# First stage of a transformer kernel taken in parts, late parameter loads moved to the next stage, and the result turned and stored in quarters between the last products

## The chip, the cores and the metric

One Trainium2 chip, of which the program uses one core. The metric is the time of one execution in device microseconds (us). Three runs of the kernel before took 1059.59, 1060.05 and 1061.69 us; the median is 1060.05 us.

The engines are called by these names: PE is TensorE (matrix products and transposes), PEld its weight loads, DVE is VectorE, ACT is ScalarE, POOL is GpSimd, SP is SyncE, which here only issues DMA transfers. A name with q (SPq, PEq) is an engine's sequencer.

## What is computed

Six blocks run one after the other on x of 256 tokens by 1024 features, all in float32: a forget-gated attention block (fox), a sparse attention block (NSA), then a gated recurrence (HGRN2), a feed-forward block, a latent attention block (MLA) and a second feed-forward block. Each adds to x. Only the two ends matter here:

```python
def rmsnorm(x, g):
    xf = x.astype(jnp.float32)
    y = xf * lax.rsqrt(jnp.mean(xf * xf, axis=-1, keepdims=True) + NORM_EPS)
    return (y * g.astype(jnp.float32)).astype(x.dtype)

def fox_mixer(h, w_in, b_f, w_out):
    proj = h @ w_in
    q, k, v, f, z = jnp.split(proj, [W, 2 * W, 3 * W, 3 * W + N_HEADS], axis=-1)
    ...
    log_f = jax.nn.log_sigmoid(f.astype(jnp.float32) + b_f.astype(jnp.float32))
    c = jnp.cumsum(log_f, axis=1).transpose(0, 2, 1)
    ...
```

The program begins with `h = rmsnorm(x, norm_g[0])` and `h @ w_in`, and ends with `x + hidden @ w_down` of the last feed-forward block, which is the output.

## The kernel before

**Layout.** x is kept turned: 128 features on the partitions, 8 chunks of features by 256 tokens. A weight tile is 1 MB, 128 x 2048 float32, that is 8 chunks of 128 rows by 256 columns. A product in float32 is made of three (`product3`, L444): both factors are split into a high part, rounded to the fast type float32r, and a low part, the remainder, and high*high, high*low and low*high are added up. So each weight tile passes through a ring of three slots: SP loads it (`load`, L356), ACT copies it to the high part (`high`, L388), DVE subtracts to get the low part (`low`, L404; `low_half`, L412, half a tile), and PE multiplies: 48 products of 128 x 256 for a tile (`by_feature`, `by_token`). SP loads the tile three places on when the low part has been taken.

**Norms.** `Norm` (L566) does not wait for the root of the mean square: it splits x times gain (`high` L577, `low` L583), multiplies, and scales the product by the row of inverse roots afterwards. For the sum, ACT squares x in four pieces (`square`, L593), POOL adds them (`add_squares`, L605), PE adds over the partitions with a column of ones (`sums`, L620), ACT takes the root (`root`, L631), DVE the inverse and a half of it (`finish`, L643), and PE spreads it over a row (`spread`, L670), which DVE copies (L664).

**Stages.** The program is a row of blocks with a function for each engine. At the end of a block all engines wait for each other. Inside a block the order of each engine is written out by hand, with semaphores between them.

**The first block (L1277 to L1350).** SP loads constants, x with tokens on the partitions, and tiles 0 to 2, then the weights of the forget gate `w_f`, its bias `b_f`, late constants and tiles 3 and 4. ACT's queue issues the load of `norm_g` and then 13 small loads of late parameters. PE runs 12 products of zeros (`keep_warm`, L553), turns the `norm_g` parameters (L1271), turns x (16 transposes, L1327), runs 12 more products of zeros, multiplies tile 0 and sums the squares. DVE copies the turned x from PSUM to SBUF (L1342), takes the low parts of h (L586), of tiles 0 and 1 (L409), and multiplies `w_f` by the gain (L1349). ACT takes the high parts of h (L580) and of tile 0 (L399), squares x (L594), takes the high part of tile 1 and loads the table of the root (L603).

**The second block (fox, from L1402)** multiplies tiles 1 to 15 (n is the tile). A function `between` or `quarter` is called after each half or quarter of a tile's products, and puts other work of PE there: the spread of the root, the product with `w_f` in three parts (`forget_product`, L1431), the running sums of the log gates (`c_sums`, L1417), the turning of their three bf16 parts (`c_turn`, L1424), and the steps of attention, from tile 3 on. The first of these waits for `c_ready`, a row that DVE copies (L1582). DVE's order there is: the gate's steps (L1555 to L1562), low part of tile 3, the split of the sums (`split_c`, L1566 to L1576), low part of tile 4, evacuation of tile 2 (L1529, L1530), the row c (L1582). POOL clears `c_parts` and `kz` (L1411, L1412) at the start of the block, and SP first loads the convolution parameters (L1262).

**The end.** In the last feed-forward block `last_down` (L1054) multiplies the last tile, two chunks of the output at a time, into banks 4 to 7; DVE adds each pair to x (L1233). Then the block ends, and a last block turns x back (16 transposes, L2910), copies four banks (L2918) and stores the result in two transfers of 512 KB (L2925).

## Time and profile before

| | us |
|---|---|
| median of three runs | 1060.05 |
| the three runs | 1059.59 to 1061.69 |
| the profiled execution, its own time | 1060.7 |
| its span, first to last instruction | 1058.9 |
| PE busy | 1021.7 (96%) |
| DVE busy | 766.7 (72%) |
| ACT busy | 549.6 (52%) |
| POOL busy | 69.7 (7%) |
| mean granted TensorE clock | 0.997 of full |

How to read it: a busy share is an average over all stages, and a matmul record runs until its modelled end, so overlapping records make PE look busy without a gap. Starts are counted from the start of the span. "Idle before" in brackets is the time in which the engine stood still before the row, and what ended it. The profiled execution took 0.65 us more than the median of the runs; 1.8 us of its time lie outside the span.

### The profile page before, as it was taken

Reading aid. Unit: us, or ns where it says so; the run is one execution under the profiler, and the core shown is the slowest. Engines: PE = TensorE matmul, PEld = TensorE weight load, DVE = VectorE, ACT = ScalarE, POOL = GpSimd, SP = SyncE. Lnnn points to the kernel's source line nnn. Section 1 sums busy time; section 2 is a strip of 40 time slices with the busy share of each in tenths; the row PEclk is TensorE's granted clock in tenths of the full one; section 3 lists DMA queues with packets and bytes.
Section 4 is the critical chain, followed back from the end, with each engine's and each line's share of the span. In section 5 each row is a group of like instructions: output and inputs, shape, how many; then the busy total and the mean of one; then the engine's idle time right before and its main releaser. Section 6 shows DMA issues by size and latency. Waiting matters only on the chain. (4 is left out here: it accounts for less than half of the span.)

```text
span 1058.9 us, 20362 instructions
## 1 busy us (share of the span) xinstructions
PE 1021.7 (96%) x8176; PEld 964.8 (91%) x8178; DVE 766.7 (72%) x1300; ACT 549.6 (52%) x869; POOL 69.7 (7%) x54
## 2 busy tenths in 40 slices
PE   7999999999899999999999999999998899999997
PEld 5988899997677999999999999999997899999997
DVE  5656676867677667498667878787866559887785
ACT  5544455455555556553555545454674555545441
POOL 4000005000000220000020000000001320000000
PEclk9999999999999999999999999999999999999999
DMA  8544345892111456600464766565531347565641
GB/s 278 160 132 144 123 127 168 225 291 82 40 41 54 146 173 187 199 1 1 138 182 121 206 190 182 175 198 160 146 119 40 93 127 210 170 200 172 198 144 40
DMA packets 184141, 153.08 MB, mean 145 GB/s; under 512 B 12477, under 2 KB 176900, under 8 KB 184068
## 3 DMA queue, kind: packets, MB, share of 16 engines
q1 hardware_dynamic: 183858, 152.01, 47.8%
q8 instruction: 51, 0.84, 0.3%
q14 instruction: 22, 0.18, 0.1%
q10 hardware_dynamic: 210, 0.05, 0.0%
HBM read 148.91 MB, written 1.05 MB: 142 GB/s over the span
## 5 line engine op out<-in xcount | busy, mean ns | idle before, releaser
L447 PE MATMUL bank<-h_high,w_high 128*128 128x256 f32 x1312 | 378.8, 289 | 6.3 <-DVE ffn_normed L1090 2.6
L448 PE MATMUL bank<-h_low,w_high 128*128 128x256 f32 x1312 | 370.9, 283 | 0.0
L449 PE MATMUL bank<-h_high,w_low 128*128 128x256 f32 x1312 | 370.9, 283 | 0.0
L399 ACT ACTIVATE w_high<-ring 128x2048 fp32r<-128x2048 f32 x137 | 261.5, 1911 | 165.4 <-PE bank L449 161.5
L409 DVE TENSOR_TENSOR w_low<-ring,w_high 128x2048 fp32r<-128x2048 f32 x118 | 271.2, 2299 | 32.8 <-ACT w_high L399 32.4
L447 PEld LDWEIGHTS bank<-h_high,w_high 128*128 128x128 f32 x1312 | 251.1, 191 | 13.5 <-issue 9.9
L448 PEld LDWEIGHTS bank<-h_low,w_high 128*128 128x128 f32 x1312 | 251.3, 192 | 0.7 <-issue 0.5
L449 PEld LDWEIGHTS bank<-h_high,w_low 128*128 128x128 f32 x1312 | 251.2, 191 | 0.0
L447 PE MATMUL bank<-ffn_hidden_high,w_high 128*128 (+1 forms) x352 | 99.8, 283 | 2.0 <-DVE ffn_hidden_low L1123 2.0
L448 PE MATMUL bank<-ffn_hidden_low,w_high 128*128 (+1 forms) x352 | 99.6, 283 | 0.0
L449 PE MATMUL bank<-ffn_hidden_high,w_low 128*128 (+1 forms) x352 | 99.6, 283 | 0.0
L1077 ACT ACTIVATE ffn_conv<-ffn_normed,par 128x256 f32<-128x256 f32 x88 | 48.0, 593 | 68.6 <-DVE ffn_normed L1090 68.4
L1099 DVE SCALAR_TENSOR_TENSOR ffn_conv<-ffn_normed,par,ffn_conv 128x254 f32<-128x254 f32 (+1 forms) x176 | 77.1, 480 | 7.4 <-ACT ffn_conv L1077 2.3
L792 ACT ACTIVATE work<-bank,work 128x128 f32<-128x128 f32 (+1 forms) x112 | 47.6, 430 | 61.6 <-DVE work L774 48.5
L611 POOL TENSOR_TENSOR h<-h 128x512 f32<-128x512 f32 x15 | 38.4, 2557 | 484.2 <-ACT h L594 483.9
L447 PEld LDWEIGHTS bank<-ffn_hidden_high,w_high 128*128 128x128 f32 x352 | 67.6, 192 | 2.3 <-issue 2.3
L449 PEld LDWEIGHTS bank<-ffn_hidden_high,w_low 128*128 128x128 f32 x352 | 67.6, 192 | 0.0
L448 PEld LDWEIGHTS bank<-ffn_hidden_low,w_high 128*128 128x128 f32 x352 | 67.6, 192 | 0.0
L774 DVE TENSOR_REDUCE work<-bank 128x2 f32<-128x256 f32 (+2 forms) x64 | 32.4, 507 | 38.1 <-PE bank L759 37.8
L754 PE MATMUL bank<-work 128*128 128x256 f32 (+2 forms) x160 | 54.2, 438 | 1.9 <-ACT work L792 1.9
L418 DVE TENSOR_TENSOR w_low<-ring,w_high 128x1024 fp32r<-128x1024 f32 x40 | 48.6, 1221 | 7.1 <-ACT w_high L399 7.0
L447 PE MATMUL bank<-w_high,h_high 128*128 128x256 f32 x160 | 46.6, 291 | 2.9 <-DVE w_low L409 2.9
(352 smaller groups left out, 1750.4 us busy)
## 6 DMA issues: line engine op xcount, KB each, us to landing
ring<-in_ffn_w_up_dram SPq DMA_DIRECT2D x44, 1024.0 KB, 6.0
ring<-in_ffn_w_down_dram SPq DMA_DIRECT2D x22, 1024.0 KB, 5.0
ring<-in_fox_w_in_dram SPq DMA_DIRECT2D x16, 1024.0 KB, 5.7
ring<-in_hgrn_w_in_dram SPq DMA_DIRECT2D x16, 1024.0 KB, 5.4
ring<-in_nsa_w_in_dram SPq DMA_DIRECT2D x14, 1024.0 KB, 5.5
ring<-in_fox_w_out_dram SPq DMA_DIRECT2D x4, 1024.0 KB, 5.0
ring<-in_nsa_w_out_dram SPq DMA_DIRECT2D x4, 1024.0 KB, 5.0
ring<-in_hgrn_w_out_dram SPq DMA_DIRECT2D x4, 1024.0 KB, 5.0
```

Source lines behind the costliest of these rows:

```text
L399: i = nc.scalar.activation(dst, src, ACT.Copy)
L409: ops.tensor_tensor(w_lo[:, t % NSLOT, :], ring[:, t % NSLOT, :], w_hi[:, t % NSLOT, :].bitcast(F32), ALU.subtract).then_inc(low_in[t % NS ...
L418: i = nc.vector.tensor_tensor(w_lo[:, t % NSLOT, q], ring[:, t % NSLOT, q], w_hi[:, t % NSLOT, q].bitcast(F32), ALU.subtract)
L447: nc.tensor.matmul(o, ah, bh, start=start, stop=False, **kw)
L448: nc.tensor.matmul(o, ah, bl, start=False, stop=False, **kw)
L449: return nc.tensor.matmul(o, al, bh, start=False, stop=stop, **kw)
L611: ops.tensor_tensor(h[:, 0:2, :], h[:, 0:2, :], h[:, 2 * i:2 * i + 2, :], ALU.add).then_inc(n_added, 1)
L754: nc.tensor.matmul(o, q, k, start=(i == 0), stop=False)
L774: i = nc.vector.tensor_reduce(least, self.bank(u), AX.X, ALU.min)
L792: i = nc.scalar.activation(pb[:, e, 0:unit["w"]], ps[:, e, :], ACT.Exp, scale=unit["scale"][1] if unit.get("scale") else -1.0, bias=self.l ...
L1077: i = nc.scalar.activation(y[:, j % 2, e, :], un[:, j % 2, e, :], ACT.Identity, scale=column(cw + 4 * FC, e, j, later), bias=column(cb, e, ...
L1099: i = nc.vector.scalar_tensor_tensor(out=dst, in0=un[:, j % 2, e, 0:S - back], scalar=column(cw + (2 - back) * 2 * FC, e, j, later), in1=d ...
```

## The change

- The first block is taken in parts. x and tiles 0 and 1 are loaded in halves, each with a semaphore. `keep_warm` runs 9, 2 and 10 products of zeros in place of 12 and 12. ACT and DVE read the turned x straight from PSUM for the high and low parts of h; the copy to SBUF comes later (`place`). Tile 0 is split in quarters, and its products wait for a quarter each.
- The norm of the first block: ACT squares x in the layout of tokens, in two instructions that also add up along the row, and takes the root. POOL's additions, PE's sums and the root in the second block are gone. The inverse is taken in the first block (`invert`), the row in the second (`take_row`). The table of the root is loaded first.
- The 13 late parameter loads move from ACT's queue in the first block to SP's queue in the second, after the load of tile 4, which moves into the second block as well. The product of `w_f` and the gain moves to DVE's second block.
- In the second block the spread comes before tile 1, the three parts of `forget_product` a quarter of a tile later, `c_sums` after three quarters of tile 2 (before: half), and `c_turn` after the first quarter of tile 3 (before: at the end of tile 2).
- The last block is gone. `turn_result` turns a pair of chunks back between the products of `last_down`, ACT copies it (`place_result`), and SP stores it: four transfers of 256 KB, in rows of 1 KB.

```diff
         def keep_warm(n):
...
-                nc.tensor.matmul(B[5][:, :], zeros_bf[:, 0:P], zeros_bf[:, :], start=True, stop=True)
+                nc.tensor.matmul(B[2][:, :], zeros_bf[:, 0:P], zeros_bf[:, :], start=True, stop=True)
...
                     elif o % 2:
                         mm.then_inc(down_done, 1)
+                    if not following and o % 2 and o > 1:
+                        turn_result(pe, o // 2 - 1)
+
+            def turn_result(pe, i):
+
+                pe.wait_ge(x_added, 4 * l + i + 1)
+                for tt in range(TT):
+                    for c in range(2):
+                        mm = nc.tensor.transpose(B[i][:, (2 * tt + c) * P:(2 * tt + c + 1) * P],
+                                                 x[:, 2 * i + c, tt * P:(tt + 1) * P], ident)
+                mm.then_inc(res_turned, 1)
+
+            def place_result(act, i):
+                act.wait_ge(res_turned, i + 1)
+                nc.scalar.activation(res[:, :, i * 256:(i + 1) * 256], B[i][:, :].rearrange("p (t d) -> p t d", t=TT),
+                                     ACT.Copy).then_inc(res_in, 1)
+
+            def store_result(sp, i):
+                sp.wait_ge(res_in, i + 1)
+                sp.dma_start(out[0].rearrange("(t p) d -> p t d", p=P)[:, :, i * 256:(i + 1) * 256],
+                             res[:, :, i * 256:(i + 1) * 256]).then_inc(stored, 16)
...
+        def fox_first(pe):
+
+            def ready(c):
+                nrm_fox.chunk(pe)(c)
+                if c == 6:
+                    in_parts(pe, f0)
+                elif c % 2 == 0:
+                    pe.wait_ge(part_low, c // 2 + 1)
...
             @block.scalar
             def _(act):
                 load_params(act, (0,), loaded_p)
-                act.wait_ge(cleared, 1)
-                n_late.append(load_params(act, (1,), loaded_p2))
-                for i in range(4):
-                    nrm_fox.high(act, i)
-                high(act, 0)
-                for i in range(4):
-                    nrm_fox.square(act, i)
-                high(act, 1)
+                act.wait_ge(cleared, 2)
                 nrm_fox.table(act)
+                act.wait_ge(p_placed, 1)
+                for c in range(DC):
+                    if c % 2 == 0:
+                        act.wait_ge(turned, c // 2 + 2)
+                    nc.scalar.activation(h_hi[:, c, :], xt(c), ACT.Copy, scale=nrm_fox.gain[:, c:c + 1])\
+                        .then_inc(n_high, 1)
+                for q in range(4):
+                    if q == 0:
+                        act.wait_ge(half_in[0], 16)
+                    if q == 2:
+                        landed(act, 0)
+                    nc.scalar.activation(quarter(w_hi, q), quarter(ring, q), ACT.Copy)\
+                        .then_inc(high_in[0] if q == 3 else part_high, 1)
+
+                def square_tokens(tt):
+                    nc.scalar.activation(h[:, 4 * tt:4 * tt + 4, :].rearrange("p c t -> p (c t)"), x_tok[:, tt, :],
+                                         ACT.Square, accum_out=rstd[:, tt:tt + 1]).then_inc(squared, 1)
...
             @block.tensor
             def _(pe):
                 pe.wait_ge(cleared, 2)
-                keep_warm(12)
+                keep_warm(9)
...
-                pe.wait_ge(x_placed, 4)
-                keep_warm(12)
+                    if c == 3:
+                        keep_warm(2)
+                keep_warm(10)
                 fox_first(pe)
-                nrm_fox.sums(pe)
 
             @block.vector
             def _(dve):
...
+                for c in range(DC):
+                    if c % 2 == 0:
+                        dve.wait_ge(n_high, c + 2)
+                    nc.vector.scalar_tensor_tensor(out=h_lo[:, c, :], in0=xt(c), scalar=nrm_fox.gain[:, c:c + 1],
+                                                   in1=h_hi[:, c, :].bitcast(F32), op0=ALU.mult,
+                                                   op1=ALU.subtract).then_inc(n_split, 1)
+                for q in range(4):
+                    dve.wait_ge(high_in[0], 1) if q == 3 else dve.wait_ge(part_high, q + 1)
+                    nc.vector.tensor_tensor(quarter(w_lo, q), quarter(ring, q), quarter(w_hi, q).bitcast(F32),
+                                            ALU.subtract).then_inc(low_in[0] if q == 3 else part_low, 1)
...
+                place(0)
+                place(1)
+                dve.wait_ge(part_high, 4)
+                low_half(dve, 1, 0, ready=True)
+                place(2)
+                low_half(dve, 1, 1)
+                place(3)
+                nrm_fox.invert(dve)
...
             @block.sync
             def _(sp):
-                n_late.append(load_params(sp, range(2, 6), loaded_p2))
+                load(sp, NSLOT + 1)
+                n_late.append(load_params(sp, range(1, 6), loaded_p2))
...
                 pe.wait_ge(narrowed, 1)
+                nrm_fox.spread(pe)
...
-                    if (n, half) == (2, 0):
-                        c_sums()
-                    if (n, half) == (2, 1):
-                        c_turn()
...
                 def quarter(n, q):
-                    if (n, q) == (1, 0):
-                        nrm_fox.spread(pe)
-                    if n == 1 and q < 3:
-                        forget_product(q)
+                    if n == 1 and q:
+                        forget_product(q - 1)
+                    if (n, q) == (2, 2):
+                        c_sums()
+                    if (n, q) == (3, 0):
+                        c_turn()
...
-                nrm_fox.finish(dve)
+                nrm_fox.take_row(dve)
+                dve.wait_ge(fl, 32)
+                nc.vector.tensor_tensor(w_f[:, :, :], w_f[:, :, :], bcast(pc("norm_g", 0, DC), 2, FOX_H),
+                                        ALU.mult).then_inc(w_f_ready, 1)
```

How the instructions stand. VectorE's first block before:

```order
L1339 COPY par<-bank 128x16 [waits params_turned]
L1342 COPY x<-bank 128x512 [waits x_turned] x4
L586 SCALAR_TENSOR_TENSOR h_low<-x,par,h_high 128x256 [waits norm_high_ready] x8
L409 TENSOR_TENSOR w_low<-ring,w_high 128x2048 [waits w_high_ready0]
L409 TENSOR_TENSOR w_low<-ring,w_high 128x2048 [waits w_high_ready1]
L1349 TENSOR_TENSOR w_f<-w_f,par 128x128 [waits fox_f_loaded]
L1277 UNCONDITIONAL_BRANCH
```

And in the change, from the last low part of h on (`bank` is the turned x in PSUM):

```order
L1442 SCALAR_TENSOR_TENSOR h_low<-bank,par,h_high 128x256
L1447 TENSOR_TENSOR w_low<-ring,w_high 128x512 [waits first_weights_high] x3
L1447 TENSOR_TENSOR w_low<-ring,w_high 128x512 [waits w_high_ready0]
L1451 COPY x<-bank 128x512 x2
L419 TENSOR_TENSOR w_low<-ring,w_high 128x1024 [waits first_weights_high]
L1451 COPY x<-bank 128x512
L419 TENSOR_TENSOR w_low<-ring,w_high 128x1024 [waits w_high_ready1]
L1451 COPY x<-bank 128x512
L666 RECIPROCAL rstd<-rstd 128x2 [waits norm_root]
L668 TENSOR_SCALAR rstd_half<-rstd 128x2 [waits norm_inverse]
L1351 UNCONDITIONAL_BRANCH
```

The four copies of x stood ahead of everything and now stand behind tile 0, up to the end of the block, and the inverse root stands behind them.

TensorE at the turning of the parts of c, tile 2 to tile 3, before:

```order
L449 MATMUL bank<-h_high,w_low 128x256
L1427 MATMUL bank<-ident_bf,work 128x128 [waits c_split_step]
L1427 MATMUL bank<-ident_bf,work 128x128
L447 MATMUL bank<-w_high,h_high 128x256 [waits bank_free1,w_low_ready0]
L448 MATMUL bank<-w_low,h_high 128x256
```

and in the change (the three rows ahead of L1538 are the last of the first twelve products of tile 3):

```order
L448 MATMUL bank<-w_high,h_high 128x256
L449 MATMUL bank<-w_low,h_high 128x256
L450 MATMUL bank<-w_high,h_low 128x256
L1538 MATMUL bank<-ident_bf,work 128x128 [waits c_split_step]
L1538 MATMUL bank<-ident_bf,work 128x128
L448 MATMUL bank<-w_high,h_high 128x256
```

The two small products moved from ahead of tile 3 to behind its twelfth product; the first attention step stands behind the twenty-fourth in both.

TensorE's end, before:

```order
L448 MATMUL bank<-ffn_hidden_low,w_high 128x256
L449 MATMUL bank<-ffn_hidden_high,w_low 128x256
L1137 UNCONDITIONAL_BRANCH
L2905 UNCONDITIONAL_BRANCH [waits barrier_Pool_Activation_PE_DVE_SP_release]
L2910 MATMUL bank<-cst,x 128x128 x16
```

and in the change:

```order
L450 MATMUL bank<-ffn_hidden_high,w_low 128x256
L1087 MATMUL bank<-cst,x 128x128 [waits ffn_added_to_x]
L1087 MATMUL bank<-cst,x 128x128 x3
L1087 MATMUL bank<-cst,x 128x128 [waits ffn_added_to_x]
L1087 MATMUL bank<-cst,x 128x128 x3
L1168 UNCONDITIONAL_BRANCH
```

Eight of the sixteen transposes stand behind the last product, and eight more, in two groups of four, now stand between the products ahead of it.

## Rows read from the trace of the kernel before

**Rows 1.** The page, busy time and share of the span by engine.

```profile
PE 1021.7 (96%) x8176; PEld 964.8 (91%) x8178; DVE 766.7 (72%) x1300; ACT 549.6 (52%) x869; POOL 69.7 (7%) x54
```

**Rows 2.** Timeline of the first 16 us: start, duration, engine, line, count, idle before.

```profile
1.50 4.16 PE L557 MATMUL bank<-zeros_bf 128*128 128x512 bf16 x12 [1.50 <-POOL eps L1295]
...
6.69 1.97 PE L1327 MATMUL bank<-cst,work 128*128 128x128 f32 x16 [0.87 <-DMA work<-in_x_dram]
...
8.11 3.30 ACT L580 ACTIVATE h_high<-x,par 128x256 fp32r<-128x256 f32 x8 [0.69 <-DVE x L1342]
...
9.78 3.25 DVE L586 SCALAR_TENSOR_TENSOR h_low<-x,par,h_high 128x256 fp32r<-128x256 f32 x8
...
13.12 2.17 ACT L594 ACTIVATE h<-x 128x512 f32<-128x512 f32 x4
...
13.24 2.29 DVE L409 TENSOR_TENSOR w_low<-ring,w_high 128x2048 fp32r<-128x2048 f32 x1 [0.21 <-ACT w_high L399]
...
15.59 0.39 PE L447 MATMUL bank<-w_high,h_high 128*128 128x256 f32 x1 [2.90 <-DVE w_low L409]
```

**Rows 3.** The same view from the last product of stage one, 21 to 25 us.

```profile
21.48 1.05 PE L627 MATMUL bank<-cst,h 128*128 128x1 f32 x8
...
23.00 0.36 PE L447 MATMUL bank<-h_high,w_high 128*128 128x256 f32 x1 [0.47 <-PEq L1277]
...
23.06 3.52 POOL L1412 MEMSET work<- 128x4096 f32 x1
...
23.48 3.13 DVE L660 TENSOR_SCALAR rstd_half<-rstd 128x2 f32<-128x2 f32 x1
...
24.50 0.60 PE L562 MATMUL bank<-cst,rstd 128*128 128x128 f32 x4
```

**Rows 4.** The same view, second to fourth tile of the fox stage, 30 to 43 us.

```profile
30.27 1.19 PE L1435 MATMUL bank<-w_f,x 128*128 128x16 f32 x10
...
32.83 0.28 PE L447 MATMUL bank<-h_high,w_high 128*128 128x256 f32 x1
...
34.27 2.29 DVE L409 TENSOR_TENSOR w_low<-ring,w_high 128x2048 fp32r<-128x2048 f32 x1
...
35.71 0.29 PE L1419 MATMUL bank<-work,cst 128*128 128x16 f32 x2
...
37.59 2.29 DVE L409 TENSOR_TENSOR w_low<-ring,w_high 128x2048 fp32r<-128x2048 f32 x1
...
39.35 0.36 PE L447 MATMUL bank<-w_high,h_high 128*128 128x256 f32 x1
...
41.22 0.42 DVE L1582 CAST work<-bank 128x256 bf16<-128x256 f32 x1
...
42.31 0.59 PE L754 MATMUL bank<-work 128*128 128x256 f32 x2
```

**Rows 5.** The same view, from the last product of the program to its end.

```profile
1051.56 0.69 DVE L1233 TENSOR_TENSOR x<-bank,x 128x512 f32<-128x512 f32 x1 [0.74 <-PE bank L449]
...
1052.57 1.94 PE L2910 MATMUL bank<-cst,x 128*128 128x128 f32 x16 [1.05 <-PEq L1137]
...
1053.23 2.48 DVE L2918 COPY work<-bank 128x512 f32<-128x512 f32 x4 [0.98 <-PE bank L2910]
...
1054.55 1.55 SPq L2925 DMA_DIRECT2D out_dram<-work  x2
```

**Rows 6.** Busy time in a stretch: length, engines, granted clock, DMA share, GB/s.

```profile
1057.50:1058.00 0.50, 0.00 (x0) 0.00 (x0) 0.00 (x0) 0.00 (x0) 0.00 (x0) 1.00 0.99 401
```

**Rows 7.** Timeline around 201.6 us, VectorE and GpSimd.

```profile
201.60 2.29 DVE L409 TENSOR_TENSOR w_low<-ring,w_high 128x2048 fp32r<-128x2048 f32 x1
...
201.74 0.53 POOL L1732 MEMSET work<- 128x512 f32 x1 [20.66 <-DVE blocks_low L2032]
```

**Rows 8.** Timeline of SyncE's queue: single issues of small loads.

```profile
9.70 2.98 SPq L1286 DMA_DIRECT2D b_f<-in_fox_b_f_dram  x1
...
22.81 0.73 SPq L1262 DMA_DIRECT2D prow<-in_ffn_conv_w_dram  x2
```

More of the change, by code:

```diff
@@ L410, in low, with low_half @@
                               ALU.subtract).then_inc(low_in[t % NSLOT], 1)
-        def low_half(dve, t, half):
+        def low_half(dve, t, half, ready=False):
             if t >= NT:
                 return
-            dve.wait_ge(high_in[t % NSLOT], t // NSLOT + 1)
+            if not ready:
+                dve.wait_ge(high_in[t % NSLOT], t // NSLOT + 1)
             q = slice(half * SLOT // 2, (half + 1) * SLOT // 2)
@@ L1146, in _ @@
                         load(sp, t)
+                    if not following:
+                        for i in range(4):
+                            store_result(sp, i)
+                        sp.wait_ge(stored, 64)
                 @block.tensor
@@ L1194, in _ @@
                     next_high(act, t0 + NTILE)
+                    if not following:
+                        for i in range(4):
+                            place_result(act, i)
                     if following:
@@ L1274, in build, with load_halves, quarter, xt @@
         f0, fz = T["fox"], T["fox_z"]
-        fox_first = tile_first(f0, by_token)(nrm_fox)
+        plan_tile(f0)
+        def fox_first(pe):
[5 more added lines that the diff above has]
+                    pe.wait_ge(part_low, c // 2 + 1)
+            w = parts(f0, "p (c n) -> p c n", c=DC, n=256)
+            for tt in range(TT):
+                for c in range(DC):
+                    if tt == 0:
+                        ready(c)
+                    mm = product3(pbank(f0)[:, tt * 256:(tt + 1) * 256],
+                                  [v[:, c, tt * P:(tt + 1) * P] for v in hsp], [v[:, c, :] for v in w],
+                                  c == 0, c == DC - 1)
+            mm.then_inc(tile_done, 1)
+        def load_halves(sp, t):
+            for half in range(2):
+                k = slice(4 * half, 4 * half + 4)
+                sp.dma_start(slot(t, DC, 256)[:, k, :], tiles[t][0][:, k, :])\
+                    .then_inc(w_loaded[t % NSLOT] if half else half_in[t], 16)
+        def quarter(r, q):
+            return r[:, 0, q * SLOT // 4:(q + 1) * SLOT // 4]
+        def xt(c):
+            return B[4 + c // 2][:, (c % 2) * S:(c % 2 + 1) * S]
         fl, w_f_ready = sem("fox_f_loaded"), sem("fox_f_weights_ready")
@@ L1287, in _ @@
                 sp.dma_start(cst[:, nfirst:], cst_dram[:, nfirst:ncst]).then_inc(loaded_c2, 16)
-                for t in range(NSLOT, NSLOT + 2):
-                    load(sp, t)
+                load(sp, NSLOT)
             @block.gpsimd
@@ L1340, in _ @@
[L1340 to L1350 removed]
+                dve.wait_ge(turned, 1)
```

115 lines of the change are left out of this document (53 added, 62 removed).

## The prediction

> **What bounds the kernel now.** I read the page first: PE is busy 96% of the span, DVE 72%, ACT 52% [rows 1]. So between the ends of the program only PE's own stream counts, and a change there gains where PE stands still or runs something that is no product. Then I read the timeline of the first 16 us [rows 2]. The reader is to see a chain in which PE multiplies nothing until 15.59: x has landed at 6.6 (PE's idle time before its transposes ends on that load), DVE copies it, ACT takes eight high parts, DVE eight low parts, ACT the high part of tile 0, DVE its low part, one whole step after the other. Next the seam of stages one and two [rows 3]: sums of squares, 1.05 us, then 0.47 us for the barrier, and tile 1 begins at 23.00. Then tiles 2 and 3 [rows 4], where the order of small work moves, and the end [rows 5]: after the last add PE waits for the barrier, turns x, DVE copies, and SP stores 1 MB, with the span ending at 1058.9. Everything between these places keeps its instructions. I take it to last as long as before; what is gained or lost at the ends goes through in full.
>
> **Stage one, up to the first product.** The 12 products of zeros take 4.16 us, the last at short spacing [rows 2]; nine end near 5.0, and the parameters are turned by 5.2. The first half of x lies between then and 6.6, when all of x had landed; I take 5.4, since it is the first half of the bytes behind the same constants. Sixteen transposes take 1.97 us, so the first pair of chunks is turned at 6.1; ACT's eight high parts at 0.41 us (3.30 for eight) then run without a gap to 9.4. The quarters of the high part of tile 0 are 128 x 512 like the four squares that took 2.17 us, so 0.54 each: 9.95, 10.5, 11.0, 11.6. DVE's low parts (3.25 for eight) follow ACT's and end at 10.3. A quarter of the low part lies between 0.57 (a quarter of 2.29 [rows 2]) and 0.69 (128 x 512 alone [rows 5]); I take 0.63. The first quarter is ready at 10.95 and the first product starts at 11.05, where it was 15.59: **4.5 us earlier**. The other quarters come every 0.63 us and PE uses one in 0.72 (six products at 0.12), so it doesn't wait again. The halves of tile 0 were not waited for before, when ACT began the tile at 11.3; that they are there at 9.4 and 10.5 is likely but unseen (rival 3).
>
> **Stage one, its end.** PE finishes 48 products, 5.76 us, at 16.8. ACT, free at 11.6, has two squares of 128 x 1024 (1.3 each with the read of the sum, an estimate from 0.54 for half the size), two halves of tile 1 (1.0 each) and a root: 16.4. DVE is later. From the last quarter, 12.8, it has four copies of x (2.48, as the four of the same form [rows 5]), two halves of a low part (2.4), the inverse and its half (0.35): 18.05. So DVE, not PE, opens the barrier, and PE stands still for 1.25 us. With the 0.47 us of the seam [rows 3] PE spreads the root at 18.5 and starts tile 1 at 19.05. Before, tile 1 began at 23.00 and lost another 0.45 to the spread inside it [rows 3]. **Gain 4.4 us**; the sums, 1.05 us, are in it. Bounds: 5.6 if DVE's tail were no longer than PE's, 2.9 if the first product came 1.5 later.
>
> **Stage two.** Three waits are at stake. First, `w_f`: its product with the gain now stands behind DVE's copy of the row, beside POOL's long memset. A DVE operation of two columns was held by that memset from 23.48 to its end, 3.13 us [rows 3]. But a subtraction of two SBUF operands ran its usual 2.29 us across another memset [rows 7], and `w_f` is of that form; so it is ready at 20.0, and PE asks at 19.05 + 2.88 = 21.9. I put 0; held, it would be ready at 22.4 and cost 0.5. Second, the removed additions of POOL and root of ACT are off the path. Third, the sums of c, **which I take as a loss**. Before, tile 1 to tile 2 took 9.83 us; now 9.35, so tile 2 starts at 28.4. The gate's product used to end at 31.46, 1.4 before tile 2 [rows 4]; now its third part ends with tile 1, at 28.55. The low part of tile 3 began 2.81 later and takes 2.29 [rows 4]: 33.65. `c_sums` starts after 36 products, at 32.7, and is done at 33.45, so the split (1.1) runs to 34.8. From the start of the low part of tile 4 to the end of the row c it was 37.59 to 41.64 [rows 4], 4.05 us: now 38.85. PE starts tile 3 at 34.8 and is at the first attention step 2.96 + 0.1 later, 37.9. Before, the row had 0.67 us to spare; now PE waits **1.0 us** (bounds: 0 if the low part of tile 3 hides better, 1.6 if the gate's steps on ACT come late). After it DVE has slack again.
>
> **The late loads.** The 13 small loads left ACT's queue before ACT had work: nothing gained. On SP they go ahead of tile 5, whose load waited until 28.9 for DVE's low part of tile 2 anyway, and now may start at 22.7. Two such issues took 0.73 us [rows 8]; 19 take 7 us from 18.8, to 25.8. Tile 5 is multiplied near 50. **0**. If this cover were gone see rival 5.
>
> **The end.** Two groups of four transposes lie between products: 0.45 each (1.94 for sixteen [rows 5]), so the last product ends 0.9 later, at 1052.4. The third group runs under DVE's last add. The add ends at 1053.15, the last group is turned at 1053.85 (1052.57 to 1053.23 for four before), ACT copies in 0.6, and SP issues at 1054.55, when it used to issue the first of two stores of 512 KB; the second went out 1.2 later [rows 5]. Data flowed at 401 GB/s up to 1058.0 [rows 6], 0.9 before the end; 1.05 MB at that rate is 2.6 us, so it began at 1055.4, 0.85 after the issue. The last quarter then flows from 1055.4 for 0.65, and the end is at 1056.95. **Gain 1.9 us**, bounds 0.6 (rate of a third) and 2.5.
>
> The Trainium skill speaks against quarters: "DMA: Bandwidth & Descriptors", section "Bandwidth", wants transfers of 1 MiB and measured 138 GB/s at 64 KB against 341 at 1 MB. By the lower figure the last quarter would flow 1.9 us (an estimate), and the gain at the end would be 0.65; no row here shows a store of this size.
>
> **Sum.** 4.4 - 1.0 + 1.9 = 5.3 us. Against the profiled execution, 1060.7, that is 1055.4; this one was 0.65 above the median of the runs, 1060.05, so the predicted median is **1054.8**.
>
> **Rivals.**
> 1. *The forecast*, 1054.8: chance 0.62.
> 2. *PE itself ends stage one.* DVE's copies and halves overlap more than I add up, and the row c isn't waited for: 5.6 + 1.9 = 7.5, so 1052.5. For it: 0.67 us to spare before. Against: DVE's list is in order, with durations from its own rows. Chance 0.10.
> 3. *The parts don't do what they say.* The first product waits for the landing of tile 0, not for its split: loads of one queue share the engines, and a half may land little before the whole. If it is there only at 11.3, the first product starts at 12.5; 1.5 is lost, and the wait for c at its bound takes 0.6 more: gain 3.2, so 1056.9. For it: all we know is that ACT found the tile there at 11.3. Chance 0.14.
> 4. *The quarters store slowly.* At a third of the rate of [rows 6] the last one flows 1.95 us, and the gain at the end is 0.6: total 4.0, so 1056.0. The page named above makes this the expected way. Chance 0.10.
> 5. *Slower: SP's queue holds the weights.* One small load, the bias, held SP for 2.98 us behind weight tiles [rows 8]. If each of the 19 did that behind tile 4, tile 5 would be issued at 18.8 + 57 = 76, not 25.8. PE can bear an issue up to about 39 (product at 50, less 6 for landing and 5 for the split); each us beyond costs one. From 44.5 the whole gain is gone, and at 76 the time is 1060 + 31 = 1092. Against: the six of stage two took under 0.4 each, the bias stood behind three tiles in flight, and now only one is. Chance 0.04.
>
> **Range and chances.** About 0.2% of the time, 2.1 us, is what a measurement here tells from no change: faster is below 1057.9. The range goes from rival 2 with a little more at the end, 1052.3, to rival 3 with the slow quarters, 1057.8. Outside it lie rival 5 and corners of the others. Faster takes rivals 1 to 4 but for their tails: 0.87. The same: tails of 3 and 4 with a wait of 0.5 for `w_f`: 0.09. Slower: rival 5: 0.04.
>
> **What would show it.** The first product of tile 0 near 11.0; DVE's last copy of x near 17.7 and PE idle for some 1.7 us before the spread; tile 1 near 19.0; the first attention step with an idle time of about 1 us that ends on the row c; the last store issued near 1051.2 (1054.55 less 3.4), and a span near 1053.6. I am wrong if DVE isn't what opens the barrier, if the wait at c is missing or over 2 us, if the last store needs over 3 us, or if PE is short of weights after tile 4.

## The result, and the profile after

| | before | changed |
|---|---|---|
| median, us (six executions each) | 1060.77 | 1054.2 |
| lowest to highest | 1059.59 to 1061.69 | 1052.91 to 1057.88 |
| profiled execution: its own time | 1060.7 | 1052.91 |
| its span | 1058.9 | 1051.1 |
| its mean granted clock of TensorE | 0.997 | 1.000 |

The ratio is 0.9944, with a 95% interval of 0.9925 to 0.9962: **faster by 5.9 us (4 to 8)**; the medians are 6.6 apart. Forecast was 1054.8, 5.3 less than before.

The busy line of the page, against [rows 1]: POOL loses the additions of the first norm (7.0 us), DVE has 6.8 us less and ACT 1.5 more.

```profile
PE 1017.8 (97%) x8167; PEld 960.9 (91%) x8167; DVE 759.9 (72%) x1300; ACT 551.1 (52%) x875; POOL 62.7 (6%) x51
```

The timeline of the first stage, rows of PE, ACT and DVE (start, length, engine, line, operation, idle time before and what ended it), against [rows 2, 3]:

```profile
6.06 1.09 PE L1426 MATMUL bank<-cst,work 128*128 128x128 f32 x8 [0.73 <-DMA work<-in_x_dram]
6.81 3.08 ACT L1389 ACTIVATE h_high<-bank,par 128x256 fp32r<-128x256 f32 x8 [4.12 <-PE bank L1426]
7.77 3.23 DVE L1442 SCALAR_TENSOR_TENSOR h_low<-bank,par,h_high 128x256 fp32r<-128x256 f32 x8 [2.24 <-ACT h_high L1389]
9.76 2.20 ACT L1396 ACTIVATE w_high<-ring 128x512 fp32r<-128x512 f32 x4
10.91 2.49 DVE L1447 TENSOR_TENSOR w_low<-ring,w_high 128x512 fp32r<-128x512 f32 x4
11.74 0.35 PE L448 MATMUL bank<-w_high,h_high 128*128 128x256 f32 x1 [0.86 <-DVE w_low L1447]
...
17.38 0.68 DVE L1451 COPY x<-bank 128x512 f32<-128x512 f32 x1
...
18.17 0.17 DVE L668 TENSOR_SCALAR rstd_half<-rstd 128x2 f32<-128x2 f32 x1
18.79 0.68 PE L563 MATMUL bank<-cst,rstd 128*128 128x128 f32 x4 [1.07 <-PEq L1351]
18.85 3.53 POOL L1523 MEMSET work<- 128x4096 f32 x1
19.97 0.29 DVE L1660 TENSOR_TENSOR w_f<-w_f,par 128x128 f32<-128x128 f32 x1
```

The chain of before, one whole step after the other, is now overlapped: ACT has begun the weights at 9.76, before DVE has ended the low parts of h. The first product is at 11.74 (15.59 before), and DVE is the last to reach the barrier, at 18.34. The product for `w_f` takes 0.29 us in the middle of POOL's memset.

Tiles 2 and 3, DVE and PE, against [rows 4]:

```profile
31.50 2.28 DVE L409 TENSOR_TENSOR w_low<-ring,w_high 128x2048 fp32r<-128x2048 f32 x1
...
32.94 0.29 PE L1530 MATMUL bank<-work,cst 128*128 128x16 f32 x2
...
34.61 0.18 DVE L1688 CAST work<-work 128x32 bf16<-128x32 f32 x1
34.83 2.29 DVE L409 TENSOR_TENSOR w_low<-ring,w_high 128x2048 fp32r<-128x2048 f32 x1
37.03 0.68 DVE L1638 TENSOR_TENSOR work<-bank,rstd_row 64x512 f32<-64x512 f32 x1
...
38.45 0.42 DVE L1694 CAST work<-bank 128x256 bf16<-128x256 f32 x1
38.93 0.70 PE L762 MATMUL bank<-work 128*128 128x256 f32 x2 [0.67 <-DVE work L1694]
```

A wait that before had not: PE stands 0.67 us at the first attention step until DVE has copied the row c. The end, against [rows 5]:

```profile
1046.53 0.69 DVE L1273 TENSOR_TENSOR x<-bank,x 128x512 f32<-128x512 f32 x1 [1.18 <-PE bank L450]
1047.27 0.66 PE L1087 MATMUL bank<-cst,x 128*128 128x128 f32 x4 [0.35 <-DVE x L1273]
1047.97 0.60 ACT L1093 ACTIVATE h<-bank 128x512 f32<-128x512 f32 x1 [0.41 <-PE bank L1087]
1048.59 0.37 SPq L1098 DMA_DIRECT2D out_dram<-h  x1
```

From the start of the last add to the end of the span it is 4.6 us, where it was 7.3.

**Where the 7.8 us between the two spans lie.** I took DVE's and ACT's instructions that both traces have, in order, and their difference in start: 3.26 us earlier from tile 3 on, 3.32 at 520, 3.59 from 527 on, then 5.88 from 839 on, and 7.8 at the end. Nothing was changed between 45 and 1040. The 0.27 us at 527 are one start of ACT (L2310 before, L2422 now), 0.37 us behind DVE's result before and 0.09 now. The late start stands in all four profiles with the old first stage and in none of the ten with the new one, so that it is gone comes with the new start; why, no run here tells. The 2.3 us between 800 and 839 are the granted clock of TensorE. Windows of before, with PE's busy time and the clock (1.00 is 2.4 GHz, 0.50 is 1.2 GHz), around the places where it fell (length, PE, clock, share of the DMA engines, GB/s):

```profile
803.00:806.00 3.00, 1.20 (x7) 1.00 0.00 0
806.50:809.90 3.40, 3.38 (x14) 0.50 0.00 0
828.00:830.00 2.00, 1.26 (x9) 1.00 0.00 0
830.40:833.80 3.40, 3.39 (x16) 0.50 0.62 184
```

In the profile of the changed kernel the clock doesn't fall. So on an even clock the change is worth 7.8 - 2.3 = 5.5 us: 3.3 at the start, 0.3 at 527, 1.9 at the end. And its six spans rise as the mean clock falls: 1051.1 at 1.000, 1051.3 and 1052.0 at 0.999, 1052.9 at 0.998, 1054.4 at 0.996, 1056.1 at 0.994.

### The profile page after: what moved, and what is told of

It is laid out like the page before. It is cut to its first block and busy times, and to the rows that moved or that the text cites. A ratio compares the mean times of both kernels' runs of the same rounds, so it can differ in the third digit from the quotient of the medians.

```text
span 1051.1 us, 20343 instructions
## 1 busy us (share of the span) xinstructions
PE 1017.8 (97%) x8167; PEld 960.9 (91%) x8167; DVE 759.9 (72%) x1300; ACT 551.1 (52%) x875; POOL 62.7 (6%) x51
## 5 line engine op out<-in xcount | busy, mean ns | idle before, releaser
L399 ACT ACTIVATE w_high<-ring 128x2048 fp32r<-128x2048 f32 x135 | 257.7, 1912 | 164.9 <-PE bank L450 157.8
L409 DVE TENSOR_TENSOR w_low<-ring,w_high 128x2048 fp32r<-128x2048 f32 x116 | 265.9, 2294 | 32.1 <-ACT w_high L399 31.8
L613 POOL TENSOR_TENSOR h<-h 128x512 f32<-128x512 f32 x12 | 31.6, 2631 | 473.7 <-ACT h L596 473.7
L419 DVE TENSOR_TENSOR w_low<-ring,w_high 128x1024 fp32r<-128x1024 f32 x42 | 51.0, 1219 | 7.1 <-ACT w_high L399 7.0
```

The lines of the kernel that those rows point to most:

```text
L399: i = nc.scalar.activation(dst, src, ACT.Copy)
L409: ops.tensor_tensor(w_lo[:, t % NSLOT, :], ring[:, t % NSLOT, :], w_hi[:, t % NSLOT, :].bitcast(F32), ALU.subtract).then_inc(low_in[t % NS ...
L419: i = nc.vector.tensor_tensor(w_lo[:, t % NSLOT, q], ring[:, t % NSLOT, q], w_hi[:, t % NSLOT, q].bitcast(F32), ALU.subtract)
L613: ops.tensor_tensor(h[:, 0:2, :], h[:, 0:2, :], h[:, 2 * i:2 * i + 2, :], ALU.add).then_inc(n_added, 1)
```

## Experiments

My theory was the prediction's own: start 3.4, end 1.9, the two independent. One rival was that the two parts hang together or that something else had given the time; another, from the comparison of the traces, that the clock was part of the change. All "even clock" figures are spans without stretches at half clock: a profile's span, less what the shift of its instructions against another profile shows for such a stretch or for a late x. For before that is 1058.9 - 2.3 = 1056.6. All runs from e6 on, and e4, start from the changed kernel.

**e1: before once more**, unchanged.

> The kernel before, once more, for the granted clock of each execution. In the profile of before, the clock stood at half for two stretches of 3.4 us near 806 and 830, in the profile of the changed kernel nowhere; the shift of DVE's and ACT's instructions between the two traces goes from 3.6 to 5.9 us across them. Theory A (those 2.3 us are chance, and the change is worth 5.5 on an even clock): the spans of before scatter from about 1056.6 (no such stretch) up, in steps that go with the mean clock, as those of the changed kernel scatter from 1051.1 at clock 1.000 to 1056.1 at 0.994; time by clock is one line for both kernels, 5.5 us apart. Theory B (the change itself removes the stretches): before never shows a clock above 0.998, and the two stretches stand at the same places in this profile.

Median 1060.06, ratio 0.9998. In this profile the clock is at half from 379.6 to 383.0, in a stage where before's first profile had none, and DVE's instructions behind it are 2.4 us later. So place and number differ from execution to execution: theory B's fixed places are wrong. Yet B was right on a point: no execution at 0.999 or above. That called for e5.

**e2: the new start with the old end. e3: the old start with the new end.** The diff of each is the other half of the change:

```diff
 # e2: as before
+                for tt in range(TT):
+                    sp.wait_ge(res_in, 2 * tt + 2)
+                    sp.dma_start(out[0, tt * P:(tt + 1) * P, :], res[:, tt, :]).then_inc(stored, 16)
 # e3: as in the change
+                        for i in range(4):
+                            store_result(sp, i)
```

> The new first stage, new order of tiles 1 to 3 and moved loads, with the end of before. My theory (start 3.3 to 3.6, end 1.9, nothing else): on an even clock the span is 1051.1 + 1.9 = 1053.0; first product 11.7, attention step 38.9 as in the profile of the changed kernel. A rival, that the two parts are not independent (the late loads or the changed places of tiles shift the ring and cost or gain something far behind): span on an even clock off 1053.0 by over 0.5.

> The old first stage, with the result turned and stored in quarters between the last products. My theory: on an even clock 1056.6 - 1.9 = 1054.7, with every instruction up to the last tile where it was before, and from the last add to the end of the span 4.6 us (1046.53 to 1051.1 in the changed kernel) where before took 7.3 (1051.56 to 1058.9). Rival, that the quarters pay only beside the new start: less than 1.5.

e2: median 1056.86, ratio 0.9960 (0.9947 to 0.9973). The profile ran at clock 1.000 with span 1054.5; the second half of x landed late, which made the start 1.42 us later, so 1053.0: as forecast. That rests on this correction; the lowest of its spans was 1053.9. e3: median 1058.18, ratio 0.9981 (0.9972 to 0.9990); its 11 spans lie between 1056.2 and 1058.4, none with a mean clock above 0.998. In its profile the clock fell in the first tile (windows as above):

```profile
14.00:17.30 3.30, 1.32 (x11) 1.00 1.01 266
17.30:20.70 3.40, 3.40 (x19) 0.50 0.90 289
```

From 23 to 806, where the clock of before falls, everything is 1.74 us later than in before: 0.39 of it because x landed late, 1.35 by that stretch. So on an even clock and with x as in before it is 1054.7: as forecast. The two halves add up: 3.9 and 2.6 us by the medians, 6.5 together.

**e4: row c ahead of the low part of tile 4.**

```diff
                 split_c()
-                low(dve, nc.vector, f0 + 4)
                 evacuate(2)
                 dve.wait_ge(c_turned, 1)
                 nc.vector.tensor_copy(c_row, B[7][:, 0:S]).then_inc(c_ready, 1)
+                low(dve, nc.vector, f0 + 4)
```

> The changed kernel, but DVE takes the evacuation of tile 2 and the row c before the low part of tile 4, not behind it. If what PE waits for at the first attention step (0.67 us, ended by the row) is only DVE's order: the row is ready at about 37.3 (turned parts at 36.9 + 0.42), PE starts the step at 38.26 without a wait and everything behind it is 0.67 earlier, as long as the low part of tile 4 (now done near 39.6) is there before PE asks for it near 41. Span on an even clock 1050.4. Rival: the low part of tile 4 or the reductions of attention are late instead, and the gain is given back within the next two tiles: 1051.1 or more.

PE and DVE of this profile, where everything up to here is 0.20 us earlier than in the changed kernel:

```profile
36.61 0.42 DVE L1693 CAST work<-bank 128x256 bf16<-128x256 f32 x1
37.06 2.29 DVE L409 TENSOR_TENSOR w_low<-ring,w_high 128x2048 fp32r<-128x2048 f32 x1
...
37.90 0.59 PE L762 MATMUL bank<-work 128*128 128x256 f32 x2
```

The step has no idle time before it, and from here on everything is 1.15 us earlier than in the changed kernel, 0.95 beyond the 0.20: the wait is DVE's order, and it is gone, with nothing late behind it in the stage. It is more than the 0.67 in the bracket, which counts from the modelled end of the product before. Without a wait the step starts 0.83 sooner, at 37.90, and its first products are 0.11 shorter. The median, 1054.74, shows none of it: the profile has three stretches at half clock (374, 804, 828), and three of the six executions stand below 0.998.

**e5: before, with more zeros ahead of the first product.**

```diff
                 pe.wait_ge(x_placed, 4)
-                keep_warm(12)
+                keep_warm(24)
```

> The kernel before, with 24 instead of 12 products of zeros behind the turned x, so that PE isn't idle for 2.9 us before the first product. So far no execution of a kernel with the old first stage (45 with its clock) had a mean clock above 0.998, and the profile with the new end alone had the clock at half from 17.3 to 20.7, after PE had been busy 1.32 of 3.3 us; of 17 with the new first stage 5 stood at 0.999 or 1.000. Theory A: that idle time is why the clock falls in the first tile, and the new first stage gains by removing it, beside its 3.3 us: here no stretch at half near 17, several executions at 0.999 or 1.000, the lowest span near 1056.6 and the median 1 to 1.4 us below that of before. Theory B, the fall near 17 has another cause or is chance: nothing above 0.998, median unchanged. The first product stays at 15.6 in both.

```profile
14.00:17.30 3.30, 2.99 (x19) 1.00 1.07 268
17.30:20.70 3.40, 3.40 (x31) 1.00 0.91 291
```

Four of 11 executions ran at 1.000, with spans of 1056.7 to 1057.1, the even clock that was worked out for before (1056.6). Of the 17 executions of before that ran beside them one did (1056.5), and of all 77 with the old first stage that same one. So the full clock was kept more often with the zeros. That they do it by preventing a fall at 17 is not shown. The same windows of the first profile of before, with PE idle from 12.69 to 15.59, have the full clock too, and so has e1:

```profile
14.00:17.30 3.30, 1.71 (x14) 1.00 1.12 280
17.30:20.70 3.40, 3.40 (x30) 1.00 0.86 284
```

There the clock fell at 806 and 830, in e1 at 380, and at 17 in e3 alone. The median of e5 is only 0.5 below that of before, and the ratio 1.0000 (0.9990 to 1.0009): the gain that I expected of it, 1 to 1.4, isn't shown. Where the clock fell in its other executions, no profile tells.

**e6: two copies of x on ACT.**

```diff
                 low_half(dve, 1, 0, ready=True)
-                place(2)
                 low_half(dve, 1, 1)
-                place(3)
 # ACT, behind its root
+                act.wait_ge(n_split, DC)
+                for i in (2, 3):
+                    nc.scalar.activation(x[:, 2 * i:2 * i + 2, :], B[4 + i][:, :]..., ACT.Copy)
```

> The changed kernel, but the last two copies of x out of PSUM are made by ACT, behind its root, not by DVE. My theory is that DVE (its last instruction ends at 18.34, PE's last product at 17.7) opens the barrier: DVE then ends near 17.2, ACT near 17.5, PE's 17.7 decides, the spread moves from 18.79 to 18.15 and tile 1 from 19.23 to 18.6; everything behind is 0.65 earlier, span on an even clock 1050.45 (for x landing when it did in the profile of the changed kernel). Rival, that it is PE's own end and the barrier takes 1.07 us: no change at 18.79.

```profile
16.23 1.07 ACT L1416 ACTIVATE x<-bank 128x512 f32<-128x512 f32 x2
...
16.91 0.17 DVE L668 TENSOR_SCALAR rstd_half<-rstd 128x2 f32<-128x2 f32 x1
...
18.12 0.57 PE L563 MATMUL bank<-cst,rstd 128*128 128x128 f32 x3 [0.47 <-PEq L1351]
```

DVE ends at 17.08, the spread stands 0.47 us behind PE's last product instead of 1.07, and all that follows is 0.67 earlier, of which 0.07 is an earlier first product: 0.60 gained. DVE did open the barrier. The median, 1055.15, is again above that of the changed kernel, with no execution above 0.998.

**e7: x in quarters**, 256 columns each, with a semaphore of its own for each.

> The changed kernel with x loaded in four parts of 256 columns, two chunks each. In the changed kernel the first half landed at 6.01 and the second 1.57 later, and PE waited 0.73 us for the first; ACT began its high parts at 6.81. If the first product hangs on the landing of x, the first quarter is there near 5.25, ACT begins at 6.1, DVE's low parts end 0.7 earlier and the first product is at 11.05 in place of 11.74; tile 1 at 18.55. Rival: shorter rows (1 KB per token) and two more issues make the load slower, the last quarter lands after 8.3 and ACT waits between its pairs: no gain or a loss.

The quarters landed at 4.32, 6.19, 6.96 and 7.65, and:

```profile
6.17 3.20 ACT L1389 ACTIVATE h_high<-bank,par 128x256 fp32r<-128x256 f32 x8 [3.48 <-PE bank L1425]
9.24 1.17 ACT L1396 ACTIVATE w_high<-ring 128x512 fp32r<-128x512 f32 x2
10.70 1.15 ACT L1396 ACTIVATE w_high<-ring 128x512 fp32r<-128x512 f32 x2 [0.29 <-DMA ring<-in_fox_w_in_dram]
...
11.10 0.36 PE L448 MATMUL bank<-w_high,h_high 128*128 128x256 f32 x1 [0.59 <-DVE w_low L1446]
```

First product 11.10, all 0.63 earlier; median 1052.67, ratio 0.9935 (0.9920 to 0.9949). Most of the 0.63 need not be the quarters': in the profile of the changed kernel the first half had landed late, at 6.01. In e9, with halves, it landed at 5.57, and ACT began its high parts at 6.38, against 6.81 there and 6.17 here. That leaves 0.2 to the quarters, and e10 doesn't show even that.

**e8: the store in one go**, two transfers of 512 KB once all four quarters are in.

```diff
-                            store_result(sp, i)
-                        sp.wait_ge(stored, 64)
+                            sp.wait_ge(res_in, i + 1)
+                        for tt in range(TT):
+                            sp.dma_start(out[0, tt * P:(tt + 1) * P, :], res[:, tt, :]).then_inc(stored, 16)
```

> The changed kernel with its transposes and copies between the last products, but the result stored in two transfers of 512 KB once all four quarters are in. If the quarters gain because only 256 KB is left to flow (0.78 us at the 336 GB/s seen for a quarter) and not by the moved transposes: 1.05 MB at the 401 GB/s of before flow 2.6 us, so the end comes 1.8 us later, span on an even clock 1052.9, and nearly all of the 1.9 us of the end are gone. If the transposes and copies were what counted: 1051.5 or less.

Span 1054.6 with one stretch at half clock, behind which everything is 1.57 later than in the changed kernel: even clock 1053.1; the one execution at 1.000 has 1053.3. Median 1055.05, ratio 0.9950 (0.9937 to 0.9964). The gain of the end, 1.9, is gone whole, so it lies in what is left to flow when the last result is there. One window of this store (its length, ACT's busy time, the clock, the DMA engines' share, GB/s) and one of the changed kernel's last quarter (with the busy times of all five engines):

```profile
1052.50:1053.00 0.50, 0.00 (x0) 0.50 1.02 418
```

```profile
1049.50:1050.00 0.50, 0.00 (x0) 0.00 (x0) 0.00 (x0) 0.00 (x0) 0.00 (x0) 1.00 0.99 336
```

**e9: tiles 0 and 1 loaded whole**, `load(sp, t)` for `load_halves(sp, t)`.

> The changed kernel with tiles 0 and 1 loaded whole (one transfer of 1 MB each), as before, and ACT and DVE still working in quarters. In the changed kernel the first half of tile 0 landed at 9.09, the second at 10.60, and ACT began its first quarter at 9.76, when its high parts of h were done. My forecast took the halves for needed; rival 3 of the prediction said that they do nothing. If a whole tile lands when its second half did: ACT begins at 10.6, the first product is at 12.55 instead of 11.74, tile 1 at 20.0, span on an even clock 1051.9. If one transfer lands sooner than two halves (9.6 as in the kernel before, where x was one transfer too): ACT isn't held, and nothing changes.

```profile
10.22 2.19 ACT L1391 ACTIVATE w_high<-ring 128x512 fp32r<-128x512 f32 x4 [0.74 <-DMA ring<-in_fox_w_in_dram]
10.88 2.50 DVE L1441 TENSOR_TENSOR w_low<-ring,w_high 128x512 fp32r<-128x512 f32 x4 [0.32 <-ACT w_high L1391]
...
11.72 0.36 PE L448 MATMUL bank<-w_high,h_high 128*128 128x256 f32 x1 [1.25 <-DVE w_low L1441]
```

The tile landed at 10.2, ACT waited 0.74 us for it and DVE 0.32 more for ACT, and yet the first product is at 11.72 as before: here h was ready 0.44 us sooner, and with halves that would have shown. So my price, 0.8, was too high; the halves are worth the 0.3 of DVE's wait here, 0.4 at most, and DVE's own work hides the rest. The span of the profile is 1051.2, as in the changed kernel; the median of the four executions is 1055.74, ratio 0.9954 (0.9939 to 0.9969), with three of them at 0.997 or 0.998.

**e10: e4, e6 and e7 together. e11: the same, with zeros in the idle places of MLA's attention.**

```diff
+                    if k in (2, 3):
+                        zeros5((2, 5)[k - 2])
...
+                    if k in (4, 16, 18):
+                        zeros5({4: 3, 16: 4, 18: 3}[k])
```

> The changed kernel with the three edits that gained: row c ahead of the low part of tile 4 (0.94 measured at the attention step), two copies of x on ACT (0.66), x in quarters (0.63). If they add up: first product 11.1, PE's last product of tile 0 at 17.05, spread at 17.5, tile 1 at 17.95, the attention step without a wait at 36.75, and the span on an even clock 1051.1 - 2.2 = 1048.9; median by chance of the clock 1.5 to 2 above it. If they stand in each other's way (ACT's two copies end after PE's last product, since ACT has 1.2 us more to do and PE ends earlier): one of the terms is halved, 1049.3.

> The kernel of the run before this one, with 17 products of zeros (0.21 us each) in the five places of the attention of MLA where PE idles: before logits 2 and 3, and before the weighing in steps 4, 16 and 18 (idle 0.54, 1.34, 0.78, 1.25 and 0.98 in the profile of the changed kernel), into a bank that nothing uses there. Three of seven profiles so far have the clock at half near 804 to 810 and 828 to 834. If PE's idle time in front is what lets the clock fall there: no such stretch in this profile, the even-clock span unchanged (1048.9), and fewer executions below clock 0.999, so a median 0.5 to 1 us lower than without the zeros. If not: the same scatter of spans and a median equal within its scatter, or higher by what the zeros delay.

e10: median 1053.12, ratio 0.9926 (0.9912 to 0.9939), profile at 1.000 with span 1049.6, not 1048.9. Behind tile 3 all is 1.63 earlier than in the changed kernel: row c and the copies gave their 0.95 and 0.60, and 0.08 came at the first product; x in quarters gave nothing: the first landed at 4.39, but PE was at its zeros until 5.45. e11: median 1051.83, ratio 0.9920 (0.9907 to 0.9934); by the shift against e10 the zeros delay nothing. That they steady the clock isn't shown: neither profile has a stretch at half before the last store, and the highest span of five is 1051.6 in both.

**e12: fewer zeros at the start**, against e11.

```diff
-                keep_warm(9)
+                keep_warm(6)
...
-                    if c == 3:
+                    if c in (1, 3):
                         keep_warm(2)
```

> The kernel of e11 with 6 instead of 9 products of zeros ahead of the turned parameters, and 2 more behind the first pair of chunks. In e7, e10 and e11 the first quarter of x landed at 4.32 to 4.41, but PE was still at its zeros (until 5.25, 5.45, 5.46; the later, the later the clock first stood at full: 4.99, 6.34, 6.93), so the first high part of ACT came at 6.2 to 6.9. If the zeros now bound the start: the parameters are turned at 4.1, the first pair at 4.5 to 5.2, the last pair follows the landing of the last quarter (7.65), ACT's high parts end near 9.0 instead of 9.9 and the first product is at 10.9 instead of 11.8; PE's last product of tile 0 at 16.7 and tile 1 at 17.75 where it was 18.7; span on an even clock 1048.6 or less. Rival: ACT (free at 17.4 with its two copies) becomes what opens the barrier, so tile 1 only gains 0.4. A second rival: with less work on PE the clock comes to full later and the first tile pays.

```profile
4.18 0.28 PE L1313 MATMUL bank<-cst,prow 16*128 16x16 f32 x1
4.39 0.88 PE L1429 MATMUL bank<-cst,work 128*128 128x128 f32 x4
...
17.21 0.68 PE L563 MATMUL bank<-cst,rstd 128*128 128x128 f32 x4 [0.53 <-PEq L1351]
```

The first product is at 10.69, the spread 1.07 us earlier than in e11. **This version has the lowest median: 1051.15 us of four executions, ratio 0.9904 (0.9886 to 0.9922)**; the interval overlaps that of e11. Its lowest span is 1049.2; by the shift of DVE's instructions against e11, 0.80 of the 1.07 us is left at 192. The stretch at half clock of its profile (373.5) hides the rest of the way; the lowest spans, 1049.2 and 1049.5, don't show the 0.8. The rival, that ACT now opens the barrier, is worth 0.06 us at most: the spread stands 0.53 behind PE's last product, where it was 0.47 in e6.

## Why the prediction was right, point by point

- **First product.** Forecast 11.05, measured 11.74; 4.5 us earlier was 3.85. The term that was mis-sized is the landing of x: I took 5.4 for the first half, it was 6.01 (PE's idle time of 0.73 ends on it). In other profiles it was 5.24 to 5.65, and there the zeros of PE bound the start instead.
- **End of stage one.** DVE ends it, as the prediction said: at 18.34 (18.05), tile 1 at 19.23 (19.05). PE stood idle for 1.07 in front of the spread, where the forecast had 1.25 and 0.47 of barrier, 1.7: PE's last product ended at 17.72, not 16.8, so DVE was only 0.6 behind it. DVE's list from the last quarter on was 0.3 shorter than I added up, which took back half of what the first product was late. Tile 2 began at 28.54, 4.29 earlier; forecast was 4.4. e6 shows the mechanism by taking it away: 0.60. Rival 2, that PE itself ends stage one, is out.
- **`w_f` beside the memset.** Costed at nothing, bound 0.5. Its 0.29 us lie inside the memset of 3.53, and PE doesn't wait for it.
- **The row c.** Forecast was a loss of 1.0, all of it a wait. `c_sums` 32.94 (32.7), end of the split 34.79 (34.8), row ready 38.87 (38.85). The idle time was 0.67, below the 1.0, since PE asked at 38.26, 0.36 later than forecast; the loss as a whole was 4.29 - 3.38 = 0.91, and e4 gave back 0.95.
- **The late loads.** Costed at nothing: 19 issues of 0.25 to 0.55 us from 19.02 to 26.5, and tile 5 issued at 26.56, where it was 28.96 before. Rival 5 is out. (Its price was added up wrongly: 37 us late, less the 5.3 gained, is 1091.7.)
- **The end.** Forecast 1.9 of gain, measured 1.9. From the last issue to the end 2.5 us (forecast 2.4), the quarter flowing at 336 GB/s in its fullest half microsecond. The Trainium skill ("DMA: Bandwidth & Descriptors", section "Bandwidth") gives 138 GB/s at 64 KB and 341 at 1 MB, measured on loads issued from GpSimd, and nothing between. This kernel's stores of 256 KB, issued from SP, are at the upper end of that, and the rule that speaks against quarters (transfers of 1 MiB or more), and rival 4 with it, didn't hold here. What the quarters do lose, against 401 GB/s in [rows 6], is a sixth of the rate on a quarter of the bytes.
- **Rival 3** said that the parts of tile 0 would do nothing. The first half landed at 9.09, the second at 10.60, ACT asked at 9.76. e9 shows that the halves of the load are worth a few tenths at most; that the gain then comes from splitting the work of ACT and DVE follows from the rows of the first stage, but no run took the split away.
- **What the prediction did not have is the clock.** I took the profiled execution of before as typical and its clock (mean 0.997) as given, so the span that it named as a sign, 1053.6, came out at 1051.1. On an even clock the gain is 5.5 (1056.6 to 1051.1), close to the 5.3 forecast, but 0.3 of it is the step at 527, in a stretch that the prediction took to last as long as before. There is luck in the median as well: its base, 1060.05 from three runs, was 0.7 below the 1060.77 of six, and the gain between the medians was 1.3 above the forecast, so the two cancelled but for 0.6. The other 1.1 of the 6.6 between the medians goes with the clock: of 77 executions with the old first stage 1 had a mean of 0.999 or more, of 42 with the new one (the changed kernel, e2, e4 and e6 to e10) 14. That a part of it comes from the start is hinted at by these counts and by e5, but the mechanism stays open. How much of the 1.1 is this and how much chance, six executions can't tell; it is within the interval.

## What to carry to other kernels

Where the start of a kernel is a chain of whole steps on three engines, cut the work into the parts in which it is used, and then add up each engine's own list up to the barrier: here PE's gain went to DVE's tail, and two copies on ACT, which had time before the barrier, gave 0.60 more. Small work that is moved later in one engine's order must be followed to its consumer, with what stands ahead of it in every queue between; exchanging two instructions was worth 0.95. Compare profiles instruction by instruction and at the same granted clock before a difference of a few us is given to a change: in this kernel the scatter from the clock (1051.1 to 1056.1) was nearly as large as the gain, and two gains of 0.95 and 0.60 us that the traces show (e4, e6) couldn't be seen in a median. Together, in e10, they show in the spans at 1.000: 1049.6 and 1050.0, against 1051.1.

## What the runs showed that I had not expected

- TensorE's clock fell to half at 17 (e3), 232 (e8), 374 to 380 (e1, e4, e6, e12), and 804 to 807 and 828 to 831 (before, e4), at some of these places in one execution and at others in the next. What brings it is open. Ahead of the falls at 17 and 806 PE had stood still for 2.9 us, and for 0.54 and 1.34. But at 374 to 380 it was only the 0.47 us of a barrier, behind 16 products of one column, and at 232 (e8) PE had no idle time at all: 32 products of 48 columns ran just ahead.

```profile
378.47 0.36 PE L447 MATMUL bank<-h_high,w_high 128*128 128x256 f32 x1 [0.47 <-PEq L1693]
```

```profile
228.34 3.67 PE L1873 MATMUL bank<-work,x 128*128 128x48 f32 x32
```

```profile
228.50:231.80 3.30, 3.30 (x33) 1.00 0.52 167
231.87:235.30 3.43, 3.43 (x18) 0.50 0.87 294
```

- By the shift of the instructions behind it one such stretch cost 0.8 us at 804, 1.35 to 1.6 at 17, 232 and 828, and 2.1 to 2.4 at 374 to 380, where PE multiplies weight tiles without a gap.
- Small steps come at full clock too. DVE's and ACT's instructions lose 0.3 us at 757 in e4 and at 264 and 757 in e6; e10, with both edits, has neither, and no run tells why.
- The start is bound by either of two things that both move: the landing of the first part of x (5.24 to 6.01 for a half) and the zeros, whose nine products take 3.65 us if the clock stands at full from 4.66, and 4.02 if only from 6.34. The second half of x landed once at 9.16 instead of 7.5, and made the whole kernel 1.4 us longer.
- Transfers by columns (1 KB of a row per token) flowed at 336 GB/s, the two of 512 KB with whole rows of 4 KB at 401 to 418.
- On DVE a subtraction (2.29) and the product for `w_f` (0.29) ran in their usual time inside POOL's memset, where in before an operation of two columns was held for 3.13 us [rows 3]. Beside POOL's additions (14.33 to 21.43 in before), which read SBUF where the memset only writes, the same two took 3.15 and 1.38; all four profiles with the old first stage have it so. Taking the additions away freed DVE as well:

```profile
14.33 7.10 POOL L611 TENSOR_TENSOR h<-h 128x512 f32<-128x512 f32 x3 [9.72 <-ACT h L594]
17.13 3.15 DVE L409 TENSOR_TENSOR w_low<-ring,w_high 128x2048 fp32r<-128x2048 f32 x1 [1.59 <-ACT w_high L399]
20.20 1.38 DVE L1349 TENSOR_TENSOR w_f<-w_f,par 128x128 f32<-128x128 f32 x1
```
